# Latent splits and rotary-key copies of the first mixer's attention handed from VectorE to GpSimd

## The reference

```python
h = x @ w_in
qa = apply_rope(h[..., :o1]...); ka = apply_rope(h[..., o1:o2]...); va = h[..., o2:o3]
out_a = dilated_mixture(qa, ka, va)                     # 8 heads of 64: attention "A"
cq = rms_norm(h[..., o3:o4], q_norm)                    # 384 latents of the queries
qb = (cq @ w_q_up).reshape(B, S, B_HEADS, B_NOPE + B_ROPE)
ckv = rms_norm(h[..., o4:o5], kv_norm)                  # 256 latents of keys and values
kv = (ckv @ w_kv_up).reshape(B, S, B_HEADS, B_NOPE + B_V)
k_pe = apply_rope(h[..., o5:]...)                       # one rotary key of 32 for all 8 heads
kb = concatenate([kv[..., :B_NOPE], broadcast_to(k_pe, (B, S, B_HEADS, B_ROPE))])
out_b = dense_attention(qb, kb, vb, ...)                # attention "B"
return concatenate([out_a, out_b]) @ w_out
```

## Time and profile before

| what | value |
|---|---|
| median of 3 runs | 2407.98 us (2407.42 to 2409.61) |
| the profiled execution, its own time | 2407.82 us |
| its span in the trace | 2406.0 us |
| mean granted clock of PE | 0.999 of full speed |
| PE busy | 2370.8 us (99%) |
| POOL busy | 1887.3 us (78%) |
| DVE busy | 1176.2 us (49%) |
| ACT busy | 702.7 us (29%) |

### The profile page before, as it was taken

One profiled execution on the slowest core, in us unless ns is written; L12 is line 12 of the kernel. 1 busy time (PEld: TensorE's weight loads), 2 busy tenths in 40 slices (PEclk: granted clock), 3 DMA queues, 4 the chain that ended last, 5 costly groups with the idle time before them and its releaser, 6 DMA issues.

```text
span 2406.0 us, 32489 instructions
## 1 busy us (share of the span) xinstructions
PE 2370.8 (99%) x11204; PEld 1851.2 (77%) x11204; DVE 1176.2 (49%) x1629; ACT 702.7 (29%) x1273; POOL 1887.3 (78%) x1565
## 2 busy tenths in 40 slices
PE   9999999999999999999999999999999999999998
PEld 7755788888878765788888778767888878678887
DVE  4686443332281777533342496646223666563224
ACT  3156242330031445333310234243010242440101
POOL 8721798889889765998898898737999988469996
PEclk9999999999999999999999999999999999999999
DMA  5200222222223110232222233212322232113322
GB/s 190 82 25 27 70 88 96 96 96 96 97 76 111 67 48 32 88 104 96 96 96 96 70 119 114 79 45 67 100 96 96 93 110 87 45 62 98 102 97 88
DMA packets 58863, 207.02 MB, mean 86 GB/s; under 512 B 6544, under 2 KB 9104, under 8 KB 58512
## 3 DMA queue, kind: packets, MB, share of 16 engines
q1 hardware_dynamic: 57472, 201.31, 25.0%
q10 hardware_dynamic: 1296, 4.39, 0.5%
HBM read 203.58 MB, written 2.10 MB: 85 GB/s over the span
## 4 chain that ended last, share of the span: by engine, by line
PE 86%; DVE 6%; POOL 4%; issue 2%; DMA 1%; ACT 1%; POOLq 0%; DVEq 0%; SPq 0%
PE bank L795 24%; PE bank L797 24%; PE bank L796 24%; PE bank L853 4%; PE bank L904 2%; PE bank L937 2%; PE bank L966 2%; POOL w_both L2996 2%; PE bank L908 1%; POOL w_both L2999 1%; PE bank L1022 1%; DVE work L2191 1%; PE bank L1066 1%; DVE work L2208 1%; DMA ring<-in_weights 1%
## 5 line engine op out<-in xcount | busy, mean ns | idle before, releaser
L2996 POOL TENSOR_TENSOR w_both<-ring,unit 128x512 fp32r<-128x512 f32 x690 | 783.1, 1135 | 368.0 <-PE bank L797 250.3
L2999 POOL TENSOR_TENSOR w_both<-ring,w_both 128x512 fp32r<-128x512 f32 x690 | 934.2, 1354 | 54.0
L795 PE MATMUL bank<-moving_hi,w_both 128*128 128x512 f32 x1834 | 719.8, 392 | 12.7 <-DVE region L2127 3.7
L797 PE MATMUL bank<-moving_hi,w_both 128*128 128x512 f32 x1834 | 714.1, 389 | 0.0
L796 PE MATMUL bank<-moving_lo,w_both 128*128 128x512 f32 x1834 | 713.9, 389 | 0.0
L795 PEld LDWEIGHTS bank<-moving_hi,w_both 128*128 128x128 f32 x1834 | 344.0, 188 | 100.1 <-issue 16.8
L797 PEld LDWEIGHTS bank<-moving_hi,w_both 128*128 128x128 f32 x1834 | 344.0, 188 | 72.9
L796 PEld LDWEIGHTS bank<-moving_lo,w_both 128*128 128x128 f32 x1834 | 344.2, 188 | 70.5 <-issue 0.7
L2941 DVE TENSOR_TENSOR region<-region,bank 128x512 f32<-128x512 f32 x64 | 39.7, 681 | 280.6 <-PE bank L797 280.6
L2094 ACT ACTIVATE region<-bank 128x512 f32<-128x512 f32 x64 | 38.3, 598 | 364.5 <-PE bank L797 364.5
L795 PE MATMUL bank<-hid_hi,w_both 128*128 (+1 forms) x352 | 137.7, 391 | 0.0
(11 more groups left out here) (396 smaller groups left out, 3735.8 us busy)
## 6 DMA issues: line engine op xcount, KB each, us to landing
ring<-in_weights SPq DMA_DIRECT2D x374, 512.0 KB, 3.2
out<-region SPq DMA_DIRECT2D x8, 256.0 KB, 2.2
x<-in_x_t SPq DMA_DIRECT2D x3, 512.0 KB, 7.8
region<-in_tables ACTq DMA_DIRECT2D x1, 1312.0 KB, 6.7
region<-in_tables ACTq DMA_DIRECT2D x1, 1024.0 KB, 5.0
region<-in_p_t ACTq DMA_DIRECT2D x2, 512.0 KB, 5.5
ring<-in_weights SPq DMA_DIRECT2D x2, 256.0 KB, 4.8
x<-in_x_t ACTq DMA_DIRECT2D x2, 256.0 KB, 5.0
```

The source lines that it names most:

```text
L795: pe.matmul(bank, lhs[0], rhs[0], start=start, stop=False, skip_group_check=True)
L797: return pe.matmul(bank, lhs[1], rhs[0], start=False, stop=stop, skip_group_check=True)
L2996: pool.tensor_tensor(w_parts[0][:, s, at], ring[:, s, at], unit[:, 0:1].broadcast_to([P, BLK // 2]), ALU.mult).then_inc(split_hi, 1)
L2999: pool.tensor_tensor(w_parts[1][:, s, at], ring[:, s, at], w_parts[0][:, s, at].bitcast(F32), ALU.subtract).then_inc(split_ready, 1)
```

## The change: what it does

DVE's list loses its last nine steps, the five splits and the four copies. POOL gets them, in two new functions that run after POOL has split weight block `("qup", 1)` and before it splits `("qup", 2)`. On POOL the hi part is a multiplication by ones instead of a cast, and the key is copied head by head, so four copies of two heads become eight of one. PE's wait for the copies counts to 8 instead of 4. DVE's copy of the last unit of attention A waits for POOL's splits, since it overwrites the first latent tile.

```diff
@@ PE, heads_ab
-                    pe.wait_ge(kpe_spread, B_HEADS // 2)
+                    pe.wait_ge(kpe_spread, B_HEADS)
@@ DVE, finish
                     dve.wait_ge(weighed, g + 1)
+                    if u == ("A", A_HEADS // 2 - 1):
+                        dve.wait_ge(parts_ready, T["parts"][("lat", 4)])
@@ DVE, latent_steps
-                for n in range(5):
-                    def split(n=n):
-                        if n == 0:
-                            dve.wait_ge(block_done, done(("qkA", 7)))
-                            dve.wait_ge(normed, T["normed"][("lat", 4)])
-                        split_here(("lat", n), n, lat[:, n, :])
-                    steps.append(split)
-                for j in range(B_HEADS // 2):
-                    def spread(j=j):
-                        dve.wait_ge(roped, ROPE_AT[("kpe",)] + 1)
-                        dve.tensor_copy(k_b[B_NOPE:B_QK, 2 * j:2 * j + 2, :], kpe[B_NOPE:B_QK, :].unsqueeze(1).broadcast_to(
-                            [B_ROPE, 2, S])).then_inc(kpe_spread, 1)
-                    steps.append(spread)
@@ POOL
+            def split_latents():
+                pool.wait_ge(block_done, done(("qkA", 7)))
+                pool.wait_ge(normed, T["normed"][("lat", 4)])
+                for n in range(5):
+                    pool.tensor_tensor(moving[0][:, n, :], lat[:, n, :], unit[:, 0:1].broadcast_to([P, S]),
+                                       ALU.mult).then_inc(hi_ready, 1)
+                    pool.wait_ge(hi_ready, T["parts"][("lat", n)])
+                    pool.tensor_tensor(moving[1][:, n, :], lat[:, n, :], moving[0][:, n, :].bitcast(F32),
+                                       ALU.subtract).then_inc(parts_ready, 1)
+            def spread_keys():
+                pool.wait_ge(parts_ready, T["parts"][("lat", 4)])
+                pool.wait_ge(roped, ROPE_AT[("kpe",)] + 1)
+                for h in range(B_HEADS):
+                    pool.tensor_tensor(k_b[B_NOPE:B_QK, h, :], kpe[B_NOPE:B_QK, :],
+                                       unit[B_NOPE:B_QK, 0:1].broadcast_to([B_ROPE, S]), ALU.mult).then_inc(kpe_spread, 1)
+                pool.wait_ge(kpe_spread, B_HEADS)
@@ POOL, main order
-                if layer:
+                if layer == 0:
+                    split_up_to(at, AT[("qup", 2)])
+                    at = AT[("qup", 2)]
+                    split_latents()
+                    spread_keys()
+                else:
```

## The result

The change makes the kernel slower. 20 runs of the changed kernel have a median of 2413.03 us (2411.48 to 2415.05), 20 of the kernel before 2409.12 (2407.19 to 2410.94): the ratio is 1.0017, with a 95% interval of 1.0011 to 1.0023, or 3.9 us between the medians. That is 0.17%, under the 0.2% that the prediction named as what a measurement can tell, but the interval leaves out 1. The forecast was +3.3 us and a range of 2408.3 to 2414.3. The span of the profiled execution is 2410.0 us, 4.0 more than before (2406.0).

What follows compares the result with a forecast made beforehand. PE, busy for 99% of the span, was taken to bound the kernel. Terms +1.1, +2.6, -0.1 and -0.3 us sum to +3.3, putting the median at 2411.3 us, range 2408.3 to 2414.3.

Steps and rivals of the forecast that it cites:

- POOL's own time: In attention A, POOL's five splits take 11.85 us and eight copies 8.3, in all 20.2; with pushes over at 140.0.
- Rivals 1 and 3: Copies on 32 partitions at 1.25 us or more, loss past 4.8 us (22%); or at 0.52, +1.9 us (6%).
- The alternation, three POOL instructions a turn: In attention A, DVE and POOL alternate by instruction; a DVE turn takes 3.7 us with splits, 3.4 to 3.9 with copies.
- Rival 2: DVE gets both heads of a turn through between two POOL instructions; stage between -0.3 and +1.5 us; 12%.
- Start, +1.1 at T(3): Turns 2 and 3: heads held behind POOL's instructions make turn 3's transposes on PE 1.1 us later, at 124.93.
- The bullet on turn 2: Turn 2: POOL gets in before head 1, which ends at 119.90; DVE and the keys' rotation are 0.78 us late.
- +2.6 (turns 4 to 7): Turns 4 to 7 of attention A, paced by DVE held behind POOL, take 15.5 us instead of 12.9.
- L: Experiments' theory: in attention A the DVE-POOL lock on SBUF operations sets the pace; late POOL start would cost +2.6 us.
- the waits of PE on L2191 in turns 4 to 7: Sign in the changed profile: PE waits for DVE's normalisation in turns 3 to 7, 4 to 5 us in all beside 2.3.
- Gain of 0.8: Attention A, if nothing else happened: DVE relieved, turns 4 to 6 at PE's 3.10 us; about 0.8 us, at most 1.1.
- The carry: Behind attention A: any stall added to PE in this stage is added to the end; rest of trace moved by 3.3 us.
- The sum: Whole kernel: +1.1 (turns 2 and 3), +2.6 (turns 4 to 7), -0.1 (turns 8 to 12), -0.3 (end) = +3.3 us.

Runs made afterwards that it cites:

- the clock held: Changed kernel with 11 unused matmuls on PE ahead of turn 3's transposes: 2411.55 us, ratio 1.0013; the same with only the splits on POOL: 2410.55 us, ratio 1.0007.
- the late variant: Changed kernel, but POOL begins the latents only when both heads of turn 3 are normalised: 2410.19 us, ratio 1.0010.
- the two kernels that have it: Changed kernel without splits, copies on POOL behind turn 15: 2407.41 us; kernel before, DVE's splits spaced into slack turns, its copies behind turn 15: 2407.88 us.

## Why the prediction was right, and where not

- **POOL's own time** (20.2 us and 1.3 of pushes, over at 140.0): right, 118.31 to 140.22. The copy on 32 partitions was taken as 1.04 us and is 1.00 undisturbed. Rivals 1 and 3, dearer and cheaper copies, are out. The Trainium skill, GPSIMD Engine Reference, section "Instruction dispatch", has every core serve its own 16 partitions of each instruction, by which 32 partitions take as long as 128; the trace agrees, 1.00 us against 1.04.
- **The alternation, three POOL instructions a turn**: right. With the clock held T(3) to T(7) takes 15.4 us against 15.5 forecast, in the late variant a turn takes 3.7 to 3.8. Rival 2, both heads between two POOL instructions, is out.
- **Start, +1.1 at T(3)**: a term too small; it is 1.4. The bullet on turn 2 let the rotation pass unheld. One of its four operations, L2135, has two SBUF inputs and was held for 0.64 us. The Trainium skill, SBUF — State Buffer, section "SBUF: two separate sides", names DVE operations with two SBUF inputs beside those in a two-port mode; I had read from the rows only that operations on PSUM pass, and the trace sides with the page, 1.34 us against 0.70.
- **"+2.6 (turns 4 to 7)"**: the right size for what L does, and not what happened in the changed kernel. There T(4) was late by 4.4 us: 1.4 stood at T(3), 0.7 is what DVE's delays alone add from T(3) to T(4) (4.00 us with the clock held, 3.28 before), and 2.3 is the half clock. T(4) to T(7) then took 9.8 us at 3.1 to 3.6 a turn, DVE's delays hidden. So the waits of PE on L2191 in turns 4 to 7, which the prediction named as a sign, are missing: all 3.3 us of such waits stand in turn 3, and DVE waits for PE from turn 5 on, not from turn 8. The step that failed is the unsaid one, that PE's clock stays at 1.0 through a longer wait. The profile before gave no price for it, but the 1.77 us of the earlier trace rows were the place to ask.
- **Gain of 0.8**: -0.60 and -0.71 by the fastest runs of the two kernels that have it, -0.9 by the length of the stage in the one of them whose clock stays up there.
- **The carry**: right; 4.2 us behind attention A, 4.0 to 4.1 near the end.
- **The sum**, +3.3 against 3.9 by medians and 4.0 in the span: near, since two delays of like size overlap. That is in part luck: the missing term is worth 0.5 to 0.7 us here, but 2.1 to 2.4 with the splits alone on POOL, where the same sum would have been wrong by as much. With the clock held, the kernel that the prediction walked through, the stage is 3.5 us longer, and the missing L2135 (0.3 at T(3)) is most of the difference to 3.3.

What stays open: in which executions the clock falls. At T(3) both profiles of the changed kernel show it, the one of the kernel before does not; about 1950 five of thirteen profiles show it behind the same wait of 2.0 us. The runs' steps fit one such fall more or less, and between profiles the one about 1950 is worth 1.5 us; that it makes the steps in the executions without a profile is argued, not shown.

## What to carry to other kernels

An idle engine is not free if its operations and those of the engine that it relieves hold each other up: look at the duration of the relieved engine's operations where both already run side by side, and count the turns in instructions of the other engine, not in shares of busy time. Before a stall on PE is made longer, read the granted clock behind the stalls that are there, in more than one profile; a fall cost between 0.5 and 2.4 us here, as much as other delays left uncovered. When two causes overlap, taking one away shows nothing of it, so take each away alone and both together before naming either.

## What the runs showed of the hardware that I had not expected

- A wait of PE of 2.6 us with 0.4 and 0.7 us around it was followed by nearly 7 us at the 1.2 GHz level; one of 3.35 us by half as long; one of 1.77 us by nothing in three profiles and in one by a mean clock of 0.57 over 4 us; one of 2.0 us, the same in thirteen profiles, by nothing in eight and by 3 to 4 us at the lower level in five, at a price of 1.5 us.
- Eleven matmuls of fp32r that nobody uses, in that wait, kept the clock at 1.00 and cost no time of their own.
- A DVE operation with two SBUF inputs that writes PSUM is held by POOL as well (1.34 us for 0.70); POOL's instruction behind it took 1.60 instead of 1.29.
